# A differential-attention stage: ratio of the softmax sums on GpSimd, VectorE's combination between two bias operations, half products copied out by VectorE

## The reference, cut to what matters

```
def one_block(args):                      # 128 queries of one head against all keys
    s = jnp.einsum('bqhcd,bkhcd->bhcqk', qblk, kf) + bias[None, :, None]
    pr = jax.nn.softmax(s, axis=-1)       # two softmaxes, c = 0 and c = 1
    w = pr[:, :, 0] - lam * pr[:, :, 1]
    return jnp.einsum('bhqk,bkhe->bqhe', w, vf)
```

## Time and profile before

| | |
|---|---|
| three runs | 1043.45, 1043.46, 1042.77 us; median 1043.45 |
| profiled execution | 1045.79 us, its span 1044.0 us |
| busy over the span | PE 1008.5 us (97%), PEld 800.3, DVE 659.5 (63%), ACT 580.8 (56%), POOL 500.5 (48%) |
| attention stage | about 449 to 760 us of the span |
| TensorE clock | granted share 1.00 in every 20 us stretch from 440 to 800 us |

### The profile page before, as it was taken

The page is one execution under the profiler, slowest core; times in us unless marked ns, Lnnn a source line. Parts: engine busy times, 40 slices in busy tenths (PEclk is TensorE's granted clock), DMA queues, the critical chain, the costliest instruction groups (busy, mean ns, idle before and its releaser), DMA issues.

```text
span 1044.0 us, 15464 instructions
## 1 busy us (share of the span) xinstructions
PE 1008.5 (97%) x5792; PEld 800.3 (77%) x5792; DVE 659.5 (63%) x1055; ACT 580.8 (56%) x890; POOL 500.5 (48%) x404
## 2 busy tenths in 40 slices
PE   8999999999999999989999999999999999999997
PEld 6877777767787888857777777777788888888886
DVE  4654958583493250259999999999966244445423
ACT  7738485744641131269999999999952221122112
POOL 1233245526566550036667767766667244354421
PEclk9999999999999999999999999999999999999999
DMA  9651543323255526839687478363285222432221
GB/s 337 241 169 36 172 147 101 116 81 115 77 162 164 159 81 188 243 101 243 167 197 210 110 192 223 82 159 122 68 300 167 86 87 86 137 121 86 100 87 41
DMA packets 105929, 150.34 MB, mean 144 GB/s; under 512 B 10232, under 2 KB 68728, under 8 KB 105848
## 3 DMA queue, kind: packets, MB, share of 16 engines
q1 hardware_dynamic: 105712, 149.36, 47.5%
q10 hardware_dynamic: 144, 0.00, 0.0%
HBM read 102.07 MB, written 44.11 MB: 140 GB/s over the span
## 4 chain that ended last, share of the span: by engine, by line
PE 63%; DVE 19%; issue 10%; ACT 3%; POOL 2%; DMA 2%; SPq 0%; DVEq 0%; POOLq 0%; ACTq 0%
DVE E_ L1638 11%; PE b_ps L1917 5%; PE b_ps L1919 5%; PE b_ps L1918 5%; PE b_ps L1814 4%; PE g_ps L1816 4%; PE g_ps L1814 4%; PE g_ps L1815 4%; PE b_ps L1815 4%; PE b_ps L1816 4%; PE o_ps L1980 3%; PE w_ps L1963 2%; PE h_ps L1814 2%; PE h_ps L1816 2%; PE h_ps L1815 2%
## 5 line engine op out<-in xcount | busy, mean ns | idle before, releaser
L1251 ACT ACTIVATE E_<-E_,nmax 128x1024 f32<-128x1024 f32 (+1 forms) x184 | 186.7, 1018 | 15.0 <-DVE nmax L1638 14.8
L1638 DVE CUSTOM_DVE_ANT_0 E_<-s_ps,bias 128x1024 f32<-128x1024 f32 (+1 forms) x184 | 188.0, 1056 | 3.6 <-PE s_ps L1930 3.6
L969 POOL TENSOR_TENSOR E_<-E_,ratio 128x576 f32<-128x576 f32 (+3 forms) x92 | 84.5, 919 | 85.8 <-DVE E_ L1654 85.8
L1816 PE MATMUL b_ps<-u_hi,wA_lo 128*128 128x512 f32 x288 | 113.3, 394 | 0.0
L972 POOL TENSOR_TENSOR E_<-E_ 128x576 f32<-128x576 f32 (+3 forms) x92 | 103.7, 1127 | 7.2
L1930 PE MATMUL s_ps<-KL,QL 128*128 128x512 f32 x256 | 90.7, 435 | 13.9 <-DVE nmax L1638 13.1
L1814 PE MATMUL b_ps<-u_hi,wA_hi 128*128 128x512 f32 x240 | 96.7, 403 | 5.0 <-DVE u_lo L1410 2.8
L1815 PE MATMUL b_ps<-u_lo,wA_hi 128*128 128x512 f32 x240 | 94.7, 395 | 0.0
L1963 PE MATMUL w_ps<-ident,E_ 128*128 128x128 f32 x624 | 83.4, 273 | 1.8 <-ACT WT L1282 1.7
L1282 ACT ACTIVATE WT<-w_ps 128x1024 f32<-128x1024 f32 (+1 forms) x96 | 83.3, 868 | 2.8 <-PE w_ps L1963 2.6
L1980 PE MATMUL o_ps<-WT,V 128*64 128x128 f32 x1280 | 84.0, 278 | 0.0
(11 more groups left out here) (228 smaller groups left out, 2329.6 us busy)
## 6 DMA issues: line engine op xcount, KB each, us to landing
QL<-qk_t SPq DMA_DIRECT2D x32, 256.0 KB, 6.9
KL<-qk_t SPq DMA_DIRECT2D x32, 256.0 KB, 8.2
bias<-line_d SPq DMA_DIRECT2D x8, 960.0 KB, 11.8
x_sb<-in_x SPq DMA_DIRECT2D x12, 512.0 KB, 9.0
z_ch<-z_stage SPq DMA_DIRECT2D x24, 256.0 KB, 2.7
qk_t<-qh SPq DMA_DIRECT2D x24, 256.0 KB, 2.3
qk_t<-ql SPq DMA_DIRECT2D x24, 256.0 KB, 2.8
mf<-mix_t SPq DMA_DIRECT2D x24, 256.0 KB, 3.8
```

Of the source, the lines that this page charges most:

```text
L1251: act.activation(e, e, ACT.Exp, bias=nmax[:, n % 5, c:c + 1], scale=-1.0, accum_out=sums[:, n % 5, c:c + 1]).then_inc(e_done, 1)
L1638: dve.tensor_tensor_reduce(weights_at(n)[:, c, 0:n_tok], s_ps[:, c, 0:n_tok], b[:, ::-1], -1.0, 3e38, ALU.add, ALU.min, nmax[:, n % 5, c:c ...
L1816: mm = pe.matmul(dst, sl, mh, start=False, stop=k == n - 1)
```

## The change

Four things are changed together:

- The ratio is no longer made by VectorE in `factor` but by GpSimd, in a new function `share(n)` ahead of its `combine(n)`. VectorE's part of the combination and GpSimd's multiply now both wait for it; GpSimd's add waits for VectorE's part.
- VectorE's `combine(n+2)` moves from ahead of `biased(n+4, 0)` to behind it.
- `half_out(j)` for the first 15 half products moves from ScalarE to the end of VectorE's iteration (ScalarE keeps the 16th and those behind the loop).
- Where a long step is followed two steps later by a long step, `split_at` goes from 448 to 512: VectorE 512 columns, GpSimd 512 in place of 576.

```diff
-            return {(1, 1): 448, (1, 0): 768, (0, 0): 256, (0, 1): 128}[(int(long_now), int(long_next))]
+            return {(1, 1): 512, (1, 0): 768, (0, 0): 256, (0, 1): 128}[(int(long_now), int(long_next))]
...
+            def share(n):
+                gp.wait_ge(r_done, n + 1)
+                if n >= 4:
+                    gp.wait_ge(w_dve, n - 3)
+                    gp.wait_ge(scaled, n - 3)
+                gp.tensor_scalar(ratio[:, n % 4:n % 4 + 1], sums[:, n % 5, 0:1], rsum[:, n % 24, 1:2], neglam[:],
+                                 ALU.mult, ALU.mult).then_inc(rr_done, 1)
+
             def combine(n):
...
-                gp.wait_ge(w_dve, n + 1)
+                gp.wait_ge(rr_done, n + 1)
                 gp.tensor_tensor(two, two, ratio[:, n % 4:n % 4 + 1].to_broadcast([P, n_tok - split_at(n)]),
                                  ALU.mult).then_inc(scaled, 1)
                 gp.wait_ge(scaled, n + 1)
+                gp.wait_ge(w_dve, n + 1)
                 gp.tensor_tensor(one, one, two, ALU.add).then_inc(w_gp, 1)
...
             for n in range(NSTEP):
                 blk, head, u, qt = STEPS[n]
+                share(n)
                 combine(n)
...
-                if half_out_at(n):
-                    half_out(halves_out(n))
                 weights_out(n)
...
                 dve.reciprocal(rsum[:, n % 24, :], sums[:, n % 5, :]).then_inc(r_done, 1)
-                dve.wait_ge(r_done, n + 1)
-                if n >= 4:
-                    dve.wait_ge(w_gp, n - 3)
-                dve.scalar_tensor_tensor(out=ratio[:, n % 4:n % 4 + 1], in0=sums[:, n % 5, 0:1],
-                                         scalar=rsum[:, n % 24, 1:2], in1=neglam[:], op0=ALU.mult, op1=ALU.mult
-                                         ).then_inc(rr_done, 1)
...
+            def half_out(j):
+                dve.wait_ge(f_mm, j + 1)
+                if j >= 2:
+                    dve.wait_ge(hp_out[j % 2], 16 * (j // 2))
+                dve.tensor_copy(hp[:, j % 2, :], half_bank(j)).then_inc(hp_done, 1)
...
                 if n + 2 < NSTEP:
                     factor(n + 2)
+                if n + 4 < NSTEP:
+                    biased(n + 4, 0)
+                if n + 2 < NSTEP:
                     combine(n + 2)
                 if n + 4 < NSTEP:
-                    biased(n + 4, 0)
                     biased(n + 4, 1)
+                if half_out_at(n):
+                    half_out(halves_out(n))
```

## The result

The changed kernel takes 1049.10 us (median; 1047.76 to 1051.03), the kernel before on the same chips 1043.46 (1042.77 to 1043.98): a ratio of 1.0061, 95% interval 1.0048 to 1.0073. The change makes the kernel 0.6% slower. The forecast was 1046.0 us, its own range 1043.5 to 1051, its sign slower; the measured change of +5.6 us is more than twice the forecast's +2.5. The profiled execution has a span of 1048.7 us against 1044.0. A kernel's time is the median of its fast executions; one of b1's four, at 3505 us, is left out.

A forecast was written before the change was run, and what follows sets the result against it. VectorE, TensorE and ScalarE were taken as nearly equally full, VectorE bounding the first stretch and TensorE the second. Terms +1.5 - 1.2 - 1.1 + 3.6 - 0.3 = +2.5 us gave 1046.0 us; range 1035.5 to 1051, the forecast's own 1043.5 to 1051.

The forecast's parts named there:

- the lock: Shared VectorE/GpSimd port: two-operand SBUF operations exclude each other, so the multiply holds VectorE's combination from 1.22 to 1.71 us.
- GpSimd's loop: Long steps: VectorE's part, signal, GpSimd's add, ratio and multiply form a cycle of 3.36 us, longer than VectorE's 3.32.
- rival 2: Attention stage: the lock does not bind, VectorE's long step is 3.03 us; about -10 us, 1033.5 us; chance 0.12.
- The ratio's time on GpSimd: Each ratio on GpSimd takes 0.34 us, bounds 0.19 and 0.42; 0.1 us more costs 6.5 us in all.
- Rival 3: The ratio is cheap on GpSimd, 0.19 to 0.27 us: -7 to -2.3 us, 1036.5 to 1041 us; chance 0.23.
- The long step: One long iteration, from VectorE's reciprocal to the next: 3.36 us after the change, where it cost 3.47.
- B, short 2 to long 3: Six iterations of heads 1 to 7: 21.6 us against 21.37, 0.2 more a head, +1.5 us in all.
- A without `wa_low`: Long 4 to short 1, heads 1, 6, 7: TensorE's 0.40 us wait goes; -0.4 a head, -1.1 us in all.
- A with `wa_low`: Long 4 to short 1, heads 2 to 5: ratios stand behind `wa_low`; +0.9 a head, +3.6 us in all.
- Rival 4: Heads 2 to 5: `wa_low` costs nothing, TensorE's slack takes it up; -1.1 us, 1042.3 us; chance 0.20.
- Head 0: First head: two iterations with 128 columns gain some 0.3 us each, five long ones 0.11; -1.2 us.
- The end: End of the attention stage: last bias operation and ScalarE's last exponentials come 0.3 us earlier, last combinations cost 0; -0.3 us.

The follow-up runs named there:

- b1: Kernel before with only the 15 half product copies moved to the end of VectorE's iteration: 1053.31 us, ratio 1.0093.
- b4: Changed kernel, but GpSimd's multiply also waits for VectorE's part of the combination, as before the change: 1057.48 us, ratio 1.0136.
- d3: Changed kernel with GpSimd making each ratio twice, the first into an unused tile: 1070.59 us, ratio 1.0247 to the kernel before.
- a2: Changed kernel with the ratio back on VectorE behind the reciprocal; order, split and copies stay changed: 1043.23 us, ratio 0.9996 to the kernel before.
- c2: Changed kernel with the ratio back on VectorE and the copies back on ScalarE: 1040.72 us, ratio 0.9971 to the kernel before.
- a3: Changed kernel with GpSimd making the next step's ratio ahead of `wa_low`: 1046.81 us, ratio 1.0038 to the kernel before.
- d2: c2 with the split back at 448 instead of 512: 1039.50 us, ratio 0.9962 to the kernel before.
- a1: Changed kernel with the 15 half product copies back on ScalarE: 1047.49 us, ratio 1.0040 to the kernel before.
- b3: Kernel before with only VectorE's combination moved between the two bias operations: 1062.04 us, ratio 1.0178.

## Why the prediction came out as it did

The sign and the range were right, and so were the three causes that the forecast named: the lock, GpSimd's loop and the ratio behind `wa_low`. The size was not: the centre lies 3.1 us too low, and of the five terms four erred to the same side. By its terms, against the table of stretches:

- **The lock holds VectorE's combination behind GpSimd's multiply** (rival 2 without it: 1033.5). Right, and shown by b4: 0.75 without a multiply beside it. In the trace of the changed kernel: 1.06 to 1.17, ending 0.55 behind the multiply, as forecast.
- **The ratio's time on GpSimd**: forecast 0.34, measured 0.342 (mean of 96). Rival 3 (0.19 to 0.27) falls. Its weight, 0.32 us a step for 0.34 of ratio, is shown by d3.
- **The long step**: forecast 3.36, measured 3.41; the loop on GpSimd is 3.42. The add starts 0.69 behind the multiply's end where 0.64 was counted: from the end of VectorE's part to the add it is 0.14 (633.73 to 633.87), not 0.09. The forecast also said that GpSimd's idle time would be nearly gone; these 0.69 us of each step are left, and its own sum for the loop contains them.
- **B, short 2 to long 3**: forecast +0.2 a head, +1.5; measured +0.35 in four heads, +0.64 in two (heads 1 and 6) and +0.2 in head 7, +2.9. Short 3 took 3.93 (forecast 3.92). In heads with `wa_low` the 0.1 a head over the forecast is long 2, with the scaling of 256 columns: 3.78, forecast 3.67. The term that was mis-sized is short 2 in heads without `wa_low`: forecast 3.92 from VectorE's work alone, measured 4.21. VectorE waits there for TensorE's scores:

```profile
698.19 0.16 DVE L1651 RECIPROCAL rsum<-sums 128x2 f32<-128x2 f32 x1
698.84 1.23 DVE L1646 CUSTOM_DVE_ANT_0 E_<-s_ps,bias 128x1024 f32<-128x1024 f32 x1 [0.49 <-PE s_ps L1942]
...
702.40 0.15 DVE L1651 RECIPROCAL rsum<-sums 128x2 f32<-128x2 f32 x1
```

  This is VectorE's timeline of the changed kernel, iteration short 2 of head 6. Short 2 takes 4.21 or 4.22 in heads 1 to 7 of a2 and c2 as well, so it is not the ratio on GpSimd that makes it. Whether that 0.49 would be there with another order on TensorE wasn't tried.
- **A without `wa_low`**: forecast -0.4 a head, -1.1; measured -0.07, -0.2. The 0.40 us of the earlier trace rows did go, but a wait came back at the transposes: TensorE waits 2.2 us in seven places for ScalarE's `weights_out`, in the list of waits above, where the kernel before has none between 460 and 745 us. Head 4 of the changed kernel, ScalarE's two lines and TensorE's:

```profile
642.01 1.15 ACT L1261 ACTIVATE E_<-E_,nmax 128x1024 f32<-128x1024 f32 x1 [0.39 <-DVE nmax L1646]
...
643.15 1.00 ACT L1292 ACTIVATE WT<-w_ps 128x1024 f32<-128x1024 f32 x1
...
644.30 1.07 PE L1975 MATMUL w_ps<-ident,E_ 128*128 128x128 f32 x8 [0.32 <-ACT WT L1292]
```

  The exponential waited 0.39 us for VectorE's bias operation of 640.75, and this stood behind the combination of 512 columns at 639.77, which the multiply held to 1.06. The hold isn't all of it: in a2 this combination takes 0.75, and the same wait is 1.5 us in seven places, with A at 16.59, where it is 16.58 here. No experiment takes that apart. "What is late next" was asked of TensorE's scores only, and not of ScalarE. Nor was it VectorE's combination of 768 columns that was held in long 4 of this head, as the forecast counted: it started 0.05 us ahead, took 1.02, and GpSimd's multiply of 256 columns was held instead, 1.44 where 0.61 was counted.
- **A with `wa_low`**: forecast +0.9 a head, +3.6; measured +0.85, +3.4. Rival 4 falls. a3 shows 2.8 us of it by moving only the ratio, a2 all.
- **Head 0**: forecast -1.2, measured -0.8. **The end**: forecast -0.3, measured +0.2. The last two combinations stand 0.48 and 1.32 us for their ratios; the first of these waits lies in the 0.2, the second behind the last reciprocal. VectorE's lines and GpSimd's multiplies beside them:

```profile
759.40 1.08 DVE L1656 SCALAR_TENSOR_TENSOR E_<-E_,ratio 128x832 f32<-128x832 f32 x1 [0.48 <-POOL ratio L970]
...
761.88 1.43 DVE L1656 SCALAR_TENSOR_TENSOR E_<-E_,ratio 128x832 f32<-128x832 f32 x1 [1.32 <-POOL ratio L970]
```

```profile
759.45 1.40 POOL L977 TENSOR_TENSOR E_<-E_,ratio 128x192 f32<-128x192 f32 x1
...
761.93 0.51 POOL L977 TENSOR_TENSOR E_<-E_,ratio 128x192 f32<-128x192 f32 x1
```

Each multiply starts 0.05 us behind the combination. The first time the multiply is held, 1.40; the second time the combination is, 1.43.

The terms as measured make -0.8 + 3.4 - 0.2 + 2.9 + 0.2 = +5.5 us, the stage's 5.52. The forecast had +2.5: 0.9 of the difference is A without `wa_low`, 1.4 B, 0.9 head 0 and the end; 0.2 goes the other way.

What the forecast didn't see at all is that the gain was within reach: it took the ratio's removal as what buys time and the order as a condition for it. a2 and c2 show the reverse. The order, together with a multiply that starts behind the ratio, gives 0.15 us in long 1 (3.47 to 3.32, d2) and with the split of 512 0.19 (3.28, c2); the ratio's move gives none of it and puts GpSimd's whole loop into VectorE's.

Open: why a1 gives back 0.25 us in A. ScalarE has the copies there again and VectorE hasn't, but which wait ends last was not followed through. It is the same between a2 and c2 (16.59 and 16.83).

## What to carry over

Before a small operation is moved to the engine with room, draw the ring that it closes: here 0.34 us on GpSimd came between VectorE's reciprocal and its own next instruction, with everything that GpSimd had ahead of it in its stream. Of two engines that share a port, look for where each one's long two-operand operation falls, and give the other something that reads PSUM to do meanwhile; a change that shifts one of them by a few tenths of a microsecond can cost or win more than the work it moves. Test the parts of a change in pairs as well as alone, the waits that it moves among them: alone all the parts that were tried lost or did nothing, and the order with the multiply waiting for the ratio alone, with either split, beat the kernel before.

## What was not expected of the hardware

- The hold at the port works both ways and is of whole instructions: GpSimd's multiply of 256 columns takes 0.61 us alone, and 1.44 when it starts 0.05 behind VectorE's combination of 768 columns (642.66 beside 642.61 in the changed kernel). A ratio on VectorE of one column took 0.22 us unheld and up to 1.49 held (b3). The Trainium skill says that the port pair is an exclusive lock for the whole instruction ("SBUF — State Buffer", section "SBUF: two separate sides"); it agrees with the runs in that such a pair never ran together. That whoever starts first has it, as the forecast took it, is so only where the starts lie clearly apart: in the changed kernel VectorE's combination starts 0.01 or 0.02 us ahead of a multiply nine times and is the one that is held each time, and 0.04 or 0.05 ahead 27 times, where GpSimd is held 24 times and VectorE 3 (the last two multiplies above show one of each).
- VectorE's operations with PSUM for an input, and the reciprocal with one input in SBUF, were not held: the bias operation at 631.46 lasts 1.20 us with the ratio and the multiply beside it, the copy 0.68 to 0.69, the reciprocal of two columns 0.15 or 0.16 with GpSimd's add beside it or without. So the same multiply costs VectorE nothing beside a bias operation and 0.3 to 0.4 us beside a combination.
- A ratio in VectorE's stream costs 0.13 us from its start to the next one's where it isn't held (628.02 to 628.15), and not the 0.39 of the earlier trace rows, which the forecast took for the ratio's own cost. In the kernel before, 55 of the 96 ratios are not held and cost 0.25 or 0.26 to the combination, which needs the ratio; so of the 0.39 some 0.13 was a hold and 0.12 the combination's wait, and the new order alone does away with the latter.
- A signal between engines is short: VectorE's combination at 615.60 starts 0.03 us behind the end of GpSimd's ratio (615.22 and 0.35), and GpSimd's add at 633.87 0.14 behind the end of VectorE's combination. What costs is the queue behind which the ratio stands.
